# A hybrid decoder layer on one core: row scale from token-major x, one transfer for the tables, zeros multiplied while x arrives, weight splits four chunks ahead, and the LRU activations ahead of a split

## The reference, cut to what matters

```python
h = rmsnorm(x, norm_g)                     # x * rsqrt(mean(x*x over channels) + eps) * g
proj = einsum('bsd,de->bse', h, w_in)      # about 4900 columns, split into the inputs of three groups
y_lru = rglru_group(...)                   # conv of width 4, two sigmoid gates, a = exp(-8 r softplus(-lam)),
                                           # h[t] = a*h[t-1] + sqrt(1-a*a)*(i*xc), times silu(z)
y_nsa = nsa_group(...)                     # 8 query heads, 2 key heads: compressed + selected + window
y_fox = fox_group(...)                     # 8 heads, causal softmax with a cumulative forget bias
return x + einsum('bse,ed->bsd', concatenate([y_lru, y_nsa, y_fox]), w_out)
```

## Time and profile before

| | us |
|---|---|
| median of three runs | 470.09 (469.82 to 470.20) |
| profiled execution | 469.13 |
| its span | 467.3 |
| PE busy | 440.6 (94%) |
| DVE busy | 306.0 (65%) |
| ACT busy | 248.4 (53%) |
| POOL busy | 74.3 (16%) |

### The profile page before, as it was taken

How to read it: one execution, slowest core, us unless ns; L and a number is a source line. 1 busy time by engine, 2 the same in 40 slices (tenths; PEclk the granted TensorE clock), 3 DMA queues, 4 the chain that set the end, 5 groups by cost and what they waited for, 6 DMA issues and landing times.

```text
span 467.3 us, 6623 instructions
## 1 busy us (share of the span) xinstructions
PE 440.6 (94%) x2328; PEld 344.1 (74%) x2328; DVE 306.0 (65%) x560; ACT 248.4 (53%) x472; POOL 74.3 (16%) x121
## 2 busy tenths in 40 slices
PE   5899999999859988999999999999899999999997
PEld 1476688788858866776677797898677778888885
DVE  6975469887897987776626873857887538722204
ACT  5555694567635585666527873862466545321100
POOL 4001240000000064545500000000065300000000
PEclk9899999999979999999999999999999999999999
DMA  8822234342131110000002126362300002842004
GB/s 262 302 91 90 90 91 135 91 110 71 45 116 66 45 47 1 2 2 1 1 1 82 58 86 181 90 177 95 132 4 3 1 9 90 295 146 91 0 1 180
DMA packets 12960, 39.52 MB, mean 85 GB/s; under 512 B 1792, under 2 KB 2048, under 8 KB 12672
## 3 DMA queue, kind: packets, MB, share of 16 engines
q1 hardware_dynamic: 12928, 39.11, 25.9%
HBM read 32.81 MB, written 2.10 MB: 75 GB/s over the span
## 4 chain that ended last, share of the span: by engine, by line
PE 78%; DVE 12%; issue 4%; ACT 3%; DMA 1%; POOL 0%; SPq 0%; DVEq 0%; ACTq 0%
PE bank L1143 12%; PE bank L1145 11%; PE bank L1144 11%; PE bank L1258 6%; PE bank L1239 5%; PE bank L1359 4%; PE bank L1361 4%; PE bank L1360 4%; PE bank L1229 3%; PE bank L1154 2%; PE bank L1230 2%; PE bank L1123 2%; PE bank L1173 2%; PE bank L1125 2%; PE bank L1124 2%
## 5 line engine op out<-in xcount | busy, mean ns | idle before, releaser
L1143 PE MATMUL bank<-xh,wh 128*128 128x512 f32 (+1 forms) x264 | 112.3, 425 | 0.0
L1145 PE MATMUL bank<-xh,wl 128*128 128x512 f32 (+1 forms) x264 | 104.1, 394 | 0.0
L1144 PE MATMUL bank<-xl,wh 128*128 128x512 f32 (+1 forms) x264 | 103.5, 392 | 0.0
L790 DVE TENSOR_TENSOR wl<-raw,wh 128x1024 fp32r<-128x1024 f32 x51 | 62.0, 1219 | 30.2 <-ACT wh L512 29.8
L512 ACT ACTIVATE wh<-raw 128x1024 fp32r<-128x1024 f32 x51 | 53.0, 1049 | 30.1 <-PE bank L1361 29.6
L985 DVE TENSOR_REDUCE negmax<-bank 128x1 f32<-128x128 f32 (+3 forms) x96 | 46.1, 485 | 22.9 <-PE bank L1231 22.4
L1143 PEld LDWEIGHTS bank<-xh,wh 128*128 128x128 f32 (+1 forms) x264 | 49.7, 188 | 14.7 <-issue 4.6
L1144 PEld LDWEIGHTS bank<-xl,wh 128*128 128x128 f32 (+1 forms) x264 | 49.6, 188 | 14.5 <-issue 4.2
L1145 PEld LDWEIGHTS bank<-xh,wl 128*128 128x128 f32 (+1 forms) x264 | 49.3, 187 | 11.8
L480 POOL TENSOR_SCALAR probs<-probs,rcp,gates 128x128 f32<-128x128 f32 (+3 forms) x44 | 26.3, 608 | 121.2 <-DVE rcp L999 121.1
L633 ACT ACTIVATE probs<-bank,negmax 128x128 f32<-128x128 f32 (+3 forms) x64 | 33.5, 527 | 14.8 <-DVE negmax L985 13.8
(11 more groups left out here) (209 smaller groups left out, 808.6 us busy)
## 6 DMA issues: line engine op xcount, KB each, us to landing
raw<-in_w_in SPq DMA_DIRECT2D x39, 512.0 KB, 3.4
raw<-in_w_out SPq DMA_DIRECT2D x12, 512.0 KB, 4.0
x_raw<-in_xT SPq DMA_DIRECT2D x8, 256.0 KB, 5.8
x_res<-in_x_tok SPq DMA_DIRECT2D x1, 2048.0 KB, 9.5
out_y<-y_out SPq DMA_DIRECT2D x8, 256.0 KB, 2.1
cmp_w_sb<-in_cmp_w SPq DMA_DIRECT2D x1, 1024.0 KB, 10.5
kh_fox<-kh_fox SPq DMA_DIRECT2D x8, 128.0 KB, 2.4
kl_fox<-kl_fox SPq DMA_DIRECT2D x8, 128.0 KB, 2.5
```

What stands on the lines that cost most here:

```text
L790: dve.tensor_tensor(wl[:, c % HL, :], raw[:, c % RAW, :], wh[:, c % HL, :].bitcast(F32), ALU.subtract).then_inc(wl_ready, 1)
L1143: pe.matmul(dst, hi, xh[:, k, :], start=(k == 0), stop=False)
L1144: pe.matmul(dst, hi, xl[:, k, :], start=False, stop=False)
L1145: mm = pe.matmul(dst, lo, xh[:, k, :], start=False, stop=(k == KT - 1))
```

## The change

- **Loads.** `chan` and `const` become one array `tables`. SP issues chunk 0, tables, x in four transfers of 512 KB, chunk 1, half of token-major x, chunk 2, the other half, then chunks 3 and 4, `lru_w`, chunk 5, `cmp_w`. (The token-major x was there already as the residual, and is still loaded for that at the end.)
- **Row scale.** ScalarE and VectorE take two token tiles each and sum their squares along the row in one instruction. Ln and Exp give a seed of the inverse root, four small VectorE instructions refine it. TensorE spreads it by four transposes at the sixth k of `project(2)`, and VectorE copies it to `rstd_bc` ahead of the first `evac`. The eight two-pass matmuls with ones, ScalarE's root and VectorE's reciprocal go.
- **Zeros.** TensorE multiplies zeros five times (128x256, float32) at the start.
- **Splits.** AHEAD is 4: `split(3)` and `split(4)` stand before the loop, `split(c+4)` in step c waits for `project(c)`. In TOKEN_MAJOR steps the splits stand behind the reads. `split_low` stands between the norm and the low parts (`after_low`), `lru_tail` behind them.
- **LRU.** The gates use two pairs of banks. `gates_of(0)` stands behind `project` of u3, 1 in the middle of fg, 2 behind it, 3 in the middle of kc. The sigmoids move one to two steps later. In step kc the last sigmoids and the whole LRU block stand ahead of `split(9)`. The forget gates get a place of their own, and `log_sigmoid` moves to step nq0. The second half of `lru_tail(2)` moves from nq0 to kw.
- `cmp_scores(0)` stands at the second k of `project` of zl0 instead of the fifth.

The diff, cut to its core:

```diff
-AHEAD = 3
+AHEAD = 4
+FIRST_SPLITS = AHEAD + 1
+RSTD_IN = AT["u", 2]
-TAIL_AT = (AT["vc", 0], AT["vc", 0], AT["ks", 0], AT["ks", 0], AT["kw", 0], AT["nq", 0], AT["vn", 0], AT["vn", 0])
+TAIL_AT = (AT["vc", 0], AT["vc", 0], AT["ks", 0], AT["ks", 0], AT["kw", 0], AT["kw", 0], AT["vn", 0], AT["vn", 0])
-STACK_LAG = 6
+STACK_LAG = 7
+        LRU_A, LRU_X = (AUX_A, MEAN), (AUX_B, NORM_W)
...
 sync
-            for k in range(KT):
-                sp.dma_start(x_raw[:, k, :], xT[:, k, :]).then_inc(x_loaded[k], 16)
+            load_w(0)
+            sp.dma_start(tab[:, :], tables).then_inc(tables_loaded, 16)
+            for k in range(KT // 2):
+                two = slice(2 * k, 2 * k + 2)
+                sp.dma_start(x_raw[:, two, :], xT[:, two, :]).then_inc(x_loaded[k], 16)
             load_w(1)
+            sp.dma_start(x_t[:, 0:2, :], x_tok[:, 0:2, :]).then_inc(x_t_loaded[0], 16)
             load_w(2)
+            sp.dma_start(x_t[:, 2:4, :], x_tok[:, 2:4, :]).then_inc(x_t_loaded[1], 16)
...
-            for c in range(4, N_STREAM + 6):
+            for c in range(6, N_STREAM + STACK_LAG):
                 load_w(c)
-                k = c - 5
+                k = c - 6
...
 scalar
+            def token_squares(t):
+                act.wait_ge(x_t_loaded[t // 2], 16)
+                act.activation(x_t[:, t, :], x_t[:, t, :], ACT.Square,
+                               accum_out=mean_sq[:, t:t + 1]).then_inc(x_sq_act, 1)
...
+            token_squares(ACT_SQUARES[0])
             split(2)
+            token_squares(ACT_SQUARES[1])
+            act.wait_ge(x_sq_act, len(ACT_SQUARES))
+            act.wait_ge(x_sq_dve, len(VECTOR_SQUARES))
+            link(act.activation(rstd_col[:, :], mean_sq[:, :], ACT.Ln, bias=eps1[:, :], scale=1.0 / D))
+            act.activation(rstd_col[:, :], rstd_col[:, :], ACT.Exp, scale=-0.5).then_inc(rms_seed, 1)
+            for c in range(3, FIRST_SPLITS):
+                split(c)
             for c in range(NSA_END):
...
                 if c >= 1:
                     norm_seeds(c - 1)
-                split(c + AHEAD)
+                if c == AT["kc", 0]:
+                    gate_sigmoids(LRU_T - 1)
+                    branch_sigmoids()
+                    lru_block()
+                if c + AHEAD >= FIRST_SPLITS and CHUNKS[c][0] not in TOKEN_MAJOR:
+                    split(c + AHEAD)
                 before(c)
                 read_tokens(c, 0, MIDDLE)
+                if AT["u", 2] <= c < AT["kc", 0]:
+                    gate_sigmoids(c - AT["u", 2])
                 if c >= 1:
-                    after(c - 1)
                     norm_high(c - 1)
                 read_tokens(c, MIDDLE, NT)
-                if c == AT["kc", 0]:
...
+                if CHUNKS[c][0] in TOKEN_MAJOR:
+                    split(c + AHEAD)
...
 vector
+            def token_squares(t):
+                dve.wait_ge(x_t_loaded[t // 2], 16)
+                dve.tensor_tensor_reduce(out=x_t[:, t, :], in0=x_t[:, t, :], in1=x_t[:, t, :], scale=1.0, scalar=0.0,
+                                         op0=ALU.mult, op1=ALU.add,
+                                         accum_out=mean_sq[:, t:t + 1]).then_inc(x_sq_dve, 1)
+            def token_rstd():
+                m, y, a = mean_sq[:, :], rstd_col[:, :], rms_tmp[:, :]
+                dve.wait_ge(rms_seed, 1)
+                link(dve.tensor_scalar(m, m, 1.0 / D, EPS, ALU.mult, ALU.add))
+                link(dve.tensor_tensor(a, y, y, ALU.mult))
+                link(dve.scalar_tensor_tensor(a, a, -0.5, m, ALU.mult, ALU.mult))
+                dve.scalar_tensor_tensor(y, a, 1.5, y, ALU.add, ALU.mult).then_inc(rcol_ready, 1)
...
             split_low(1)
+            token_squares(VECTOR_SQUARES[0])
+            split_low(2)
+            token_squares(VECTOR_SQUARES[1])
+            token_rstd()
...
-            dve.reciprocal(rstd_bc[:, :], rstd_bc[:, :]).then_inc(rstd_ready, 1)
-            split_low(2)
+            for c in range(3, FIRST_SPLITS):
+                split_low(c)
+            dve.wait_ge(rstd_T, 1)
+            link(dve.tensor_copy(rstd_bc[:, :], AUX_B[:, :]))
             for c in range(NSA_END):
...
                 if c >= 1:
                     after(c - 1)
+                if CHUNKS[c][0] == "zl":
+                    cmp_transposed(CHUNKS[c][1])
+                if c + AHEAD >= FIRST_SPLITS and CHUNKS[c][0] not in TOKEN_MAJOR:
+                    split_low(c + AHEAD)
+                if c >= 1:
+                    after_low(c - 1)
...
                 for i, step in enumerate(TAIL_AT):
                     if step == c:
                         lru_tail(i // 2, i % 2)
-                split_low(c + AHEAD)
+                if CHUNKS[c][0] in TOKEN_MAJOR:
+                    split_low(c + AHEAD)
...
 tensor
+                    if k == KT - 3 and c == RSTD_IN:
+                        spread_rstd()
+                    if k == KT // 2:
+                        if c == AT["fg", 0]:
+                            gates_of(1)
+                        if c == AT["kc", 0]:
+                            gates_of(3)
...
+            def spread_rstd():
+                pe.wait_ge(rcol_ready, 1)
+                for t in range(NT):
+                    mm = pe.transpose(AUX_B[:, t * P:(t + 1) * P], rstd_col[:, t:t + 1].broadcast_to([P, P]), ident)
+                mm.then_inc(rstd_T, 1)
...
-            for k in range(KT):
...
-                pe.matmul(MEAN[:, :], ones[:, :], square, start=(k == 0),
-                          stop=(k == KT - 1)).then_inc(x_sq_used, 1)
+            pe.wait_ge(zeros_ready, 1)
+            for _ in range(5):
+                pe.matmul(PT[0][:, 0:2 * P], v_blocks[:, 0, 0:P], v_blocks[:, 1, :], start=True, stop=True)
```

More of the change, by code:

```diff
@@ L83, with program @@
 FIRST_Z = AT["zn", 0]
-TAIL_AT = (AT["vc", 0], AT["vc", 0], AT["ks", 0], AT["ks", 0], AT["kw", 0], AT["nq", 0], AT["vn", 0], AT["vn", 0])
+TAIL_AT = (AT["vc", 0], AT["vc", 0], AT["ks", 0], AT["ks", 0], AT["kw", 0], AT["kw", 0], AT["vn", 0], AT["vn", 0])
 OUT_ORDER = (2, 1, 0, 3)
-STACK_LAG = 6
-POOL_SQUARES = (1, 3, 5)
-VECTOR_SQUARES = tuple(k for k in range(KT) if k not in POOL_SQUARES)
+STACK_LAG = 7
+ACT_SQUARES = (0, 2)
+VECTOR_SQUARES = (1, 3)
 GAIN = {"ks": "ks_g", "kw": "kw_g", "nq": "nq_g", "fq": "fq_g", "fk": "fk_g"}
-def program(nc, xT, x_tok, w_in, w_out, chan, const, lru_w, cmp_w, out):
+def program(nc, xT, x_tok, w_in, w_out, tables, lru_w, cmp_w, out):
     ctx = ExitStack()
@@ L191, in program @@
         OUT = (bank[2], bank[3])
-        x_loaded = [sem(f"x_loaded{k}") for k in range(KT)]
-        const_loaded, chan_loaded = sem("const_loaded"), sem("chan_loaded")
+        x_loaded = [sem(f"x_loaded{k}") for k in range(KT // 2)]
+        x_t_loaded = [sem(f"x_t_loaded{k}") for k in range(NT // 2)]
+        tables_loaded = sem("tables_loaded")
         lru_w_loaded, cmp_w_loaded = sem("lru_w_loaded"), sem("cmp_w_loaded")
@@ new lines, in branch_sigmoids, with lru_block @@
+            def branch_sigmoids():
+                act.wait_ge(proj_read, proj_units(AT["fg", 0]) + 1)
+                b = ch("fg_b")
+                act.activation(fg_sig, fg_in, ACT.Sigmoid, bias=b[0:64]).then_inc(fg_act, 1)
+                link(act.activation(fg_abs, fg_in[0:HEADS], ACT.Abs, bias=b[0:HEADS]))
+            def lru_block():
+                act.wait_ge(lru_tau, LRU_T)
+                act.wait_ge(conv_done, LRU_T)
+                for j in range(LRU_T):
+                    act.activation(u_pad[:, j, 0:SEQ], tau[:, j, :], ACT.Sqrt, scale=4.0).then_inc(lru_sqrt, 1)
+                act.preload_act_table_set("natural_log_exp_and_others")
+                link(act.activation(fg_abs, fg_abs, ACT.Exp, scale=-1.0))
+                act.activation(fg_abs, fg_abs, ACT.Ln, bias=one1[0:HEADS, :]).then_inc(fg_act, 1)
+                for j in range(LRU_T):
+                    act.wait_ge(lru_ix, j + 1)
+                    link(act.activation(xc[:, j, :], tau[:, j, :], ACT.Ln, bias=one1[:, :]))
+                    act.activation(xc[:, j, :], xc[:, j, :], ACT.Exp, scale=-1.0).then_inc(lru_seed, 1)
@@ L647, in _ @@
             act.preload_act_table_set("natural_log_exp_and_others")
-            act.wait_ge(chan_loaded, 16)
+            act.wait_ge(tables_loaded, 16)
             act.wait_ge(small_consts, 1)
+            split(0)
+            for k in range(KT):
+                act.wait_ge(x_loaded[k // 2], 16)
+                act.activation(xh[:, k, :], x_raw[:, k, :], ACT.Copy, scale=ch("norm_g", k)).then_inc(xh_ready, 1)
+            split(1)
             lam = chn[:, CH["lam"]:CH["lam"] + LRU_T]
@@ L707, in _ @@
                 norm_seeds(c - 1)
-                split(c + AHEAD)
+                if CHUNKS[c][0] not in TOKEN_MAJOR:
+                    split(c + AHEAD)
                 before(c)
@@ L1410, in pack @@
         "w_out": w_out[0].reshape(ET, P, D),
-        "chan": chan, "const": constants(), "lru_w": lru, "cmp_w": cmp,
```

(1 more changed line is left out.)

164 lines of the change are left out of this document (53 added, 111 removed).

## The result

The changed kernel takes 474.66 us (median; 473.58 to 475.09), beside 470.01 for the kernel before on the same chip (469.82 to 470.20): a ratio of 1.0096, 95% interval 1.0076 to 1.0115. It is slower by 4.6 us, where the forecast was 1.2 us slower (471.3, range up to 473.6). The sign was right; the time lies outside the range. The profiled execution took 473.58 us, span 471.8, 4.45 more than that of before.

The account below looks back on a forecast made before the run. TensorE, busy 94%, was taken as the bound, losing time in waits, most at the start. Lead after chunk kw -0.15, +0.5 to the attention, -1.6 at its start: 1.25 us slower, 471.3 beside the median; range 466.6 to 473.6.

Parts of the forecast that it names:

- x and `project(1)`: At the start: x arrives from 7.1 us on, VectorE's `xl` sets the pace, and `project(1)` starts at 14.5 us.
- inside the wait for `evac(0)`: At the start: a 1.2 GHz clock in `project(0)` moves `project(1)` by 1.2 us, hidden while TensorE waits for `evac(0)`.
- The scale itself: Row scale at the start: token-major x lands at 18.9 us, squares take 1.25, and `evac(0)` is done at 27.15.
- 8.2 us of lead: End of `project(kc)`: TensorE 8.2 us ahead of the kernel before, since all gates are then behind it.
- g: End of the last LRU gates on TensorE: 47.75 us, where it was 52.65 before, so 4.9 us ahead.
- evac(ks) and the head mean: VectorE queues behind the LRU block: evac(ks) at g + 22.8, head mean at g + 24.2; TensorE stands 6.3 us.
- The clock behind it: Behind TensorE's wait at the head mean of ks: the clock falls and costs 2.0 us, bounds 1.4 and 2.9.
- From there to the first zl step: From chunk kw to the attention: TensorE is the bound, net +0.5 us from the vn chunk, the 4.9 us wait unchanged.
- Rival A: Between ks and the first zl: VectorE, not TensorE, carries the time, so the kernel is faster, 466.6 us; chance 0.20.
- The start of the attention: `split(22)` ahead of the sigmoid's table load: first exp 4.48 us behind the last zl matmul, before 2.87; cost 1.6 us.
- Behind that: After the attention's start, chunks fq to zn and output projection: nothing is late, price 0, at most 0.5 us either way.
- Rival C: Start: reducing square takes twice as long or x lands late, `project(3)` at 28.7, clock low longer: 473.7; shared chance 0.17.

Follow-up runs that it names:

- the combination: Kernel after with low parts of chunks 9 and 10 behind evac(ks), chunk 22's split behind the nsa attention, twelve multiplications of zeros, 448 unused bytes: 463.09 us.

## Why the prediction was off

Its steps against the trace, in the order of the sum:

- **x and `project(1)`: failed.** `project(1)` started at 16.96 for 14.5. 0.95 of that is x, used from 8.05 for 7.1; VectorE kept its pace and had low part 1 done at 15.45. The other 1.5 are `project(0)` at 1.2 GHz. The prediction named that price (1.2 us) and put it "inside the wait for `evac(0)`". The cover was only 1.25 us (27.15 - 25.9), and x and the clock together used 2.5. So there was no such wait: `project(3)` ran back to back with `project(2)`, at 28.60 for 27.15, and the `evac(0)` that was to hold it waited for TensorE's own transposes instead (the copy of the spread scale, 0.80 us of waiting). With twelve zeros, the clock kept, `project(3)` did start at 26.93, on the heels of `evac(0)`. The scale itself was right: the second half of token-major x was used at 19.22 for 18.9, its sums ended 1.16 (ScalarE) and 1.23 us (VectorE) later, with their reads, for 1.25. The 8.2 us of lead at the end of `project(kc)` don't follow from the prediction's own terms (4.9 + 2.75 = 7.65); the sum doesn't use them.
- **g**, the end of the last gates: 49.43 for 47.75, the 1.45 us above and 0.2 of the longer step.
- **evac(ks) and the head mean: right.** g + 22.8 and g + 24.2 were forecast; 72.23 and 73.62 are g + 22.8 and g + 24.2, and the steps between came as listed, so this is not luck: the high part of chunk 9 was ready at g + 15.7 (15.65 forecast). The 12 us of VectorE and the 6.0 us of TensorE (6.3 forecast) stand where it put them.
- **The clock behind it: right**, 2.1 us for 2.0 (from the head mean to `compress(0)` 5.15 us, for 3.02 before). Lateness at `compress(0)`: 2.1 us, for 0.15; another 0.15 of that is the 73.80 of the chain, taken for the head mean's time before, which is 73.63 in the timeline.
- **From there to the first zl step:** 0.3 us won, for 0.5, but by other parts: 0.3 was lost on the way, where 0.5 should have been won, and the wait itself was 0.65 shorter, where nothing was forecast. Rival A, that VectorE carries this stretch, is refuted: with 7 us of lead the wait of the first zl step stayed at 4.3.
- **The start of the attention: right.** TensorE came to it 2.0 us late and was 3.6 late behind its wait: 1.6, as forecast. (The step from the first zl step to here lost another 0.2.) The Trainium skill (ScalarE: Activation LUTs, What ACT_TABLE_LOAD costs) would have made it 3.0 with its drain; here each load took 1.28 us, it began within 0.02 us of the end of the activation ahead of it, and the next activation began 1.29 and 1.30 us after its start, so the trace does not agree with the drain.
- **Behind that: failed, small.** 0 was forecast, bounds 0.5, and 0.9 us were lost: 0.2 in the nsa attention, 0.3 in the chunks fq to zn, whose step is longer, 0.4 in the fox attention and 0.2 in the last chunks; the output projection, at 0.2324 for 0.2333, gave 0.3 back. In both attentions the clock was low where it was not before (in the stretches above), and the prediction has no term for it.

The miss of 3.2 us is thus 1.7 at the start, 0.3 at the head mean of ks (0.1 clock, 0.15 the time before), 0.3 from there to the attention, 0.9 behind it. The first is a cover that was counted without its own clock: a wait of one engine was used to hide another's delay, when the two ended 1.25 us apart. Of the last two the step of 0.2325 is a part, which no part of the prediction could see, since it took the tiles' addresses to be free. Another part is the low clock in the attentions, and that isn't shown to come from the change: the low stretch in the fox attention is in 11 of the 14 traces here, also in that of the kernel before with shifted tiles, and the one in the nsa attention in 4, all with a wait of 2.3 us at its start, as three traces without it also have. Rival C's time (473.7, just outside the stated range) and its 28.7 for `project(3)` came out nearest, by luck: its squares that take twice as long did not happen. What the prediction did not ask is the question with the largest answer: the low parts ahead of `evac(ks)` cost 7.6 us, and nothing needed them there.

## What to carry to other kernels

Before engines are made earlier, look at each one's queue between two evacuations: an instruction that waits for a block on another engine holds all behind it, and it turns a lead of TensorE into a wait, and the wait into a lower clock. The waits of 4.3 to 6.0 us here each cost between 1.6 and 3.7 us more behind themselves; where one can't be removed, give TensorE something to multiply, until the operand is there. When a tile is added or removed, compare the step between matmuls in both traces before the order of work is blamed.

## What the runs showed of the hardware

**The address of a tile changes a full-rate matmul.** 128x512 float32r matmuls follow one another in 0.2286 to 0.2290, 0.2324 or 0.2333 us, by nothing but the addresses of the SBUF tiles, and which property of an address counts is open. The Trainium skill (TensorE: Matmul & The Clock Gate, Wait — 56ns, not 53.3ns?) has one figure for a warm matmul of 512 columns, 215.7 ns; no chunk of any kernel here ran at it, and the measurement decides.

**The lower clock lasts differently behind equal waits.** Behind the wait of 4.3 us of the first zl step the granted clock was 0.50 for about 6 us in the kernel after, 9 with twelve zeros, and 3 in the combination:

```profile
131.00:134.00 3.00, 3.00 (x13) 2.81 (x13) 2.86 (x7) 1.58 (x3) 0.00 (x0) 0.50 0.34 109
```

What it cost goes with the part of the low stretch that lies behind the first transposes (read off the granted clock microsecond by microsecond), of which about half is lost in these four traces: some 3 us cost 1.6 (second transposes after 9.17 us, for 7.58 with the wait filled), 5 cost 2.4, 7 cost 3.2 (the low parts moved), 8 cost 3.7 (twelve zeros). What decides where the stretch lies and how long it is stays open.
